# GpSimd makes the low halves of the activations in the second expert table's stage, VectorE only those of the weights

## The chip, the cores and the metric

The kernel runs on one core of a Trainium2 chip. The time is device microseconds of one launch of the whole program. Below, PE is TensorE, DVE is VectorE, ACT is ScalarE, POOL is GpSimd and SP is SyncE, whose queue issues most of the transfers.

## The reference

Two transformer blocks run on 256 tokens of width 1024, in 32-bit floating point. The first is an mLSTM mixer, an MLP and a gated per-layer embedding; the second is a forgetting attention beside an RWKV-7 time mix, then a layer of experts (PEER). The change is in the last part of that layer:

```
h = jax.nn.gelu(jnp.einsum('thkd,td->thk', u_table[idx], xb), approximate=False)
return jnp.einsum('thk,thkd->td', gate * h, v_table[idx])
x = _layer_norm(DN_ALPHA * x + _peer(x, ...), ln2_g[l], ln2_b[l])
```

There are 128 x 128 = 16384 experts, each with a row of `u_table` and a row of `v_table`. Every token chooses 16 experts in each of 8 heads. The kernel does not gather the rows. It computes the product of every expert with every token, multiplies it by a gate that is zero for the experts that were not chosen, and multiplies the result with the whole `v_table`.

## The kernel before

Every weight matrix is cut into items of 128 x 1024 numbers, 512 KB each, 442 in all. An item lands in one of four slots of the ring `RAW` (issued on SP's queue). Each fp32 product is made out of three faster matmuls: a number is split into a high half (rounded to the format fp32r) and a low half (the number less its high half), and high x high, low x high and high x low are summed in PSUM. So an item needs two more tiles of its own slot: `WH`, a cast on ACT, and `WL`, the subtraction `RAW - WH`. The semaphore `w_hi` counts the casts, `w_lo` the subtractions, and `w_used` the items that PE has finished. SP loads item n when item n-4 has been subtracted; ACT casts it when it has landed and PE has finished item n-4.

Up to the end of the first expert table (`u`, 128 items) POOL makes every `WL` (`split_low`, L335 to L340). After its last one POOL has no more work.

The stage of the second expert table (`v_table`, the last 128 items, here called 0 to 127) works otherwise. The left operand is the gated activation `HS[:, j, :]`, 128 experts x 256 tokens, and it has to be split too, into `CH` (a cast on ACT, `c_high`, L719 to L723) and `CL = HS - CH` (`c_low`, L785 to L789), each with four slots. For an item j, ACT makes `WH` and then `CH`; DVE makes `WL` (`v_low`, L1807 to L1811) and then `CL`; PE (`v_item`, L1191) waits for `w_lo` and for `cl_ready` and then runs 12 matmuls of 512 columns into four PSUM banks that gather the sum over all 128 items. The queues are in program order on each engine, and the loops are written out by hand:

- Entry. DVE's last gating work of the table before ends, then it runs `v_low(0)`, `c_low(0)`, `v_low(1)`, `c_low(1)` and so on to 3. `WH` of items 0 to 3 was already cast while DVE was still gating. ACT casts `CH` 0 to 3 only after the last gating, as `HS` is not final before it.
- First half, items 0 to 63. Only half of `HS` was gated in the table before. The gates of the other half (j from 64) come back from DRAM in 32 blocks into `stage`, fetched on ACT's queue, and DVE multiplies them in (`gate_rest`, L1779 to L1783), two blocks for every four items, ahead of the four `v_low` and `c_low` of the round.
- Middle, item 64. ACT casts `WH` of items 64 to 67, each of which waits for PE to finish the item four before it, then waits for the last `gate_rest`, issues the load of the saved residual, and only then casts `CH` of items 64 to 67 in a row.
- Second half, items 68 to 127. `WH`, `CH`, `WL`, `CL` for each item, nothing else.

At the end DVE and ACT do the last layer norm.

Of the kernel before, what the change touches and what calls it, by code (L numbers as in the profile page):

```python
# [19 lines left out]
ALU = mybir.AluOpType  # L20
# [30 lines left out]
PH, NK, TOPK = 8, 128, 16  # L51
# [16 lines left out]
RING = 4  # L68
# [35 lines left out]
def bass_blocks(nc, weights, x_in, p_in, vec_in, rows_in, gate_w_in, lora_in, mb_in, fb_in, out, rest_dram, x2_dram):  # L104
    with ExitStack() as ctx:
# [3 lines left out]
        def at(name, shape, dt, offset):  # L109
            return nc.alloc_sbuf_tensor_at(name, shape, dt, offset=base + offset)  # L110
# [100 lines left out]
        HS = at("HS", [P, NK, S], F32, A0)  # L211
# [22 lines left out]
        CH = at("CH", [P, RING, S], F32R, 8192)  # L234
        CL = at("CL", [P, RING, S], F32R, 12288)
# [9 lines left out]
        def sem(name):  # L245
            if name not in sems:
                sems[name] = ctx.enter_context(nc.semaphore(name))
            return sems[name]
# [8 lines left out]
        def plain(ap):  # L257
            return ap.bitcast(F32)
# [4 lines left out]
        @block.sync  # L263
        def _(sp):
            sp.dma_start(H[:, :, :], x_in.rearrange("(t p) d -> p t d", p=P)).then_inc(sem("x_landed"), 16)
            for n in range(RING):
                sp.dma_start(RAW[:, n, :], weights[n]).then_inc(w_landed[n], 16)
            full = (N_ITEMS // RING) * RING
            with sp.Fori(1, N_ITEMS // RING) as i:
                for slot in range(RING):  # L270
                    n = i * RING

                    sp.wait_ge(w_lo, n + (slot + 1 - RING))
                    sp.dma_start(RAW[:, slot, :], weights[bass.ds(n + slot, 1)].rearrange("a p d -> p (a d)")).then_inc(w_landed[slot], 16)
            for n in range(full, N_ITEMS):
                sp.wait_ge(w_lo, n + 1 - RING)
                sp.dma_start(RAW[:, n % RING, :], weights[n]).then_inc(w_landed[n % RING], 16)
            for t in range(NT):
                sp.wait_ge(sem("y_ready"), t + 1)
                sp.dma_start(out[t * P:(t + 1) * P, :], H[:, t, :]).then_inc(sem("y_stored"), 16)  # L280
            sp.wait_ge(sem("y_stored"), 16 * NT)


        @block.gpsimd
        def _(pool):
            made = sem("pool_made")
            count = [0]

            def link(ins):

                count[0] += 1
                ins.then_inc(made, 1)
                pool.wait_ge(made, count[0])

            def keep(view, pattern, base, cm, op, fill=0.0):
                link(nc.gpsimd.affine_select(out=view, in_=view, compare_op=op, fill=fill, base=base,  # L296
                                             pattern=pattern, channel_multiplier=cm))

            link(nc.gpsimd.memset(ident[:, :], 1.0))
            keep(ident[:, :], [[-1, P]], 0, 1, ALU.is_equal)  # L300
            nc.gpsimd.memset(ones_row[:, :], 1.0).then_inc(sem("ident_ready"), 1)
            link(nc.gpsimd.memset(sel4[:, :, :], 1.0))
            keep(sel4[:, :, :], [[-1, MH], [0, P]], 0, 1, ALU.is_equal)
            link(nc.gpsimd.memset(sel8[:, :, :], 1.0))
            keep(sel8[:, :, :], [[-1, FH], [0, P]], 0, 1, ALU.is_equal)

            link(nc.gpsimd.memset(mask_m[:, :, :, :], 1.0))
            for sb in range(NT):
                keep(mask_m[:, 0, sb, :], [[1, S]], -sb * P, -1, ALU.is_ge)
                keep(mask_m[:, 1, sb, :], [[-1, S]], sb * P, 1, ALU.is_ge)  # L310

            link(nc.gpsimd.memset(mask_f[:, :], 0.0))
            keep(mask_f[:, :], [[-1, S]], P, 1, ALU.is_ge, NEG)

            link(nc.gpsimd.memset(mask_r[:, :], 1.0))
            for half in range(2):
                v = mask_r[64 * half:64 * half + 64, :]
                keep(v[:, 0:64], [[1, 64]], -1, -1, ALU.is_ge)
                keep(v[:, 64:128], [[1, 64]], 0, -1, ALU.is_ge)
            link(nc.gpsimd.memset(blk_ones[:, :], 0.0))  # L320
            link(nc.gpsimd.memset(blk_ones[0:64, 0:64], 1.0))
            link(nc.gpsimd.memset(blk_ones[64:128, 64:128], 1.0))
            link(nc.gpsimd.memset(blk16[:, :], 1.0))
            for half in range(2):
                v = blk16[64 * half:64 * half + 64, :]
                keep(v, [[-BLK, 64 // BLK], [0, BLK]], 0, 1, ALU.is_ge)
                keep(v, [[BLK, 64 // BLK], [0, BLK]], BLK - 1, -1, ALU.is_ge)
            link(nc.gpsimd.memset(resets[:, :], 1.0))
            link(nc.gpsimd.memset(resets[:, :].rearrange("p (c t) -> p c t", t=CH_T)[:, :, 0:1], 0.0))
            link(nc.gpsimd.iota(iota_f[:, :], [[1, P]], base=0, channel_multiplier=0,  # L330
                                allow_small_or_imprecise_dtypes=True))
            link(nc.gpsimd.memset(eps_c[:, 1:2], GN_EPS))
            nc.gpsimd.memset(eps_c[:, 0:1], 1.0).then_inc(sem("consts_ready"), 1)

            def split_low(n, slot):  # L335


                pool.wait_ge(w_hi, n + 1)  # L338
                nc.gpsimd.tensor_tensor(WL[:, slot, :], RAW[:, slot, :], plain(WH[:, slot, :]),  # L339
                                        ALU.subtract).then_inc(w_lo, 1)  # L340

            full = FIRST["v_table"] // RING
            with pool.Fori(0, full) as i:  # L343
                for slot in range(RING):
                    split_low(i * RING + slot, slot)
            for n in range(full * RING, FIRST["v_table"]):
                split_low(n, n % RING)


        @block.scalar  # L350
        def _(act):
# [237 lines left out]
            for k, (_, _, dst, adds, _) in enumerate(INVERSE):  # L589
                if adds:  # L590
                    continue
                for half in range(2):
                    act.wait_ge(sem(f"inv_mm{half}"), k + 1)
                    b = 4 * (1 - half) + 2 * (k % 2)
                    nc.scalar.copy(inv[half][dst][:, :, :].rearrange("p u n -> p (u n)"),
                                   PS[:, b:b + 2, :].rearrange("p b n -> p (b n)")).then_inc(
                                       sem(f"inv_copied{half}"), 1)
# [615 lines left out]
        def _(dve):  # L1213
            V = nc.vector
# [564 lines left out]
            def gate_rest(i, b):  # L1779

                dve.wait_ge(sem(f"fetched{b}"), 16 * i + 16)
                hs = HS[:, NK // 2:NK, tokens(16 * i + 8 * b, 8)]
                V.tensor_tensor(hs, hs, stage[:, b, :, :], ALU.mult).then_inc(sem("rest_gated"), 1)  # L1783

            def c_low(j, c):

                dve.wait_ge(sem("ch_ready"), j + 1)
                hs = HS[:, j, :] if isinstance(j, int) else HS[:, bass.ds(j, 1), :].rearrange("p a s -> p (a s)")
                V.tensor_tensor(CL[:, c, :], hs, plain(CH[:, c, :]), ALU.subtract).then_inc(sem("cl_ready"), 1)  # L1789


            wait("u_bank_free", NT + NK // 4)
            wait("x2_stored", 16)
# [13 lines left out]
            def v_low(j, c):  # L1807

                slot = (FIRST["v_table"] + c) % RING
                dve.wait_ge(w_hi, j + (FIRST["v_table"] + 1))  # L1810
                V.tensor_tensor(WL[:, slot, :], RAW[:, slot, :], plain(WH[:, slot, :]), ALU.subtract).then_inc(w_lo, 1)  # L1811
# [2 lines left out]
            dve.wait_ge(w_lo, FIRST["v_table"])  # L1814
            for c in range(4):
                v_low(c, c)
                c_low(c, c)
            with dve.Fori(0, S // 16) as i:
                for b in range(2):
                    gate_rest(i, b)  # L1820
                for c in range(4):
                    v_low(4 * i + RING + c, c)
                    c_low(4 * i + RING + c, c)
            with dve.Fori(S // 16 + 1, NK // 4) as i:
                for c in range(4):
                    v_low(4 * i + c, c)
                    c_low(4 * i + c, c)

            used(N_ITEMS - 1)
            wait("x2_back", 16)  # L1830
# [76 lines left out]
```

## Time and profile before

| | |
|---|---|
| median of 3 runs | 1645.95 us (1644.81 to 1646.76) |
| the profiled execution, its own time | 1643.69 us |
| its span, from the first to the last instruction | 1641.6 us |
| outside the span | 2.09 us |
| PE, DVE, ACT and POOL busy | 1519.2, 869.9, 750.6 and 777.8 us |
| the stage of the second expert table, first to last matmul | 1276.54 to 1628.9 us |

The span is longer than any engine's busy time, so an engine's own total does not tell what sets the end. Busy PE is not PE at its peak, as matmuls are pipelined; where they follow each other without a gap, PE is what the rest waits for. The page gives POOL no busy time in the last quarter of the span.

### The profile page before, as it was taken

The numbers are of one execution on the slowest core, as the hardware profiler recorded it, in microseconds if no ns is written. First come the engines' busy times: TensorE is split into PE (matmuls) and PEld (weight loads), VectorE is DVE, ScalarE is ACT, GpSimd is POOL, SyncE is SP. The second block draws the span as 40 slices with busy tenths as digits, with TensorE's granted clock in tenths as the row PEclk, the third lists the DMA queues.
The fourth block names the chain that finished last, engine by engine and source line by source line (L and its number), as shares of the span: only waits on it lengthen the run. The fifth ranks groups of instructions, "written<-read, shape, count | busy, mean of one in ns | idle before, by whom it ended". The sixth has DMA issues, their size and how long they took to land.

```text
span 1641.6 us, 28210 instructions
## 1 busy us (share of the span) xinstructions
PE 1519.2 (93%) x9610; PEld 1360.0 (83%) x9610; DVE 869.9 (53%) x1889; ACT 750.6 (46%) x1064; POOL 777.8 (47%) x346
## 2 busy tenths in 40 slices
PE   6987999987999798977999999999999999999996
PEld 5766999865997568855999999999999788878885
DVE  3234442012927643234249980688888666665554
ACT  5354555344448223233456666333333444545543
POOL 6834688865776300125769998666664000000000
PEclk9998999998999668988999999999999999999998
DMA  4532455544454200015445556555554777766562
GB/s 165 181 101 81 138 181 192 192 142 140 153 169 134 83 1 1 27 40 166 167 149 171 185 167 197 167 169 177 172 179 147 262 243 242 248 219 193 191 195 85
DMA packets 74644, 254.99 MB, mean 155 GB/s; under 512 B 8409, under 2 KB 8793, under 8 KB 74330
## 3 DMA queue, kind: packets, MB, share of 16 engines
q1 hardware_dynamic: 63632, 231.76, 43.7%
q10 hardware_dynamic: 10954, 22.43, 4.0%
q8 instruction: 40, 0.66, 0.2%
q14 instruction: 18, 0.15, 0.0%
HBM read 243.67 MB, written 10.49 MB: 155 GB/s over the span
## 4 chain that ended last, share of the span: by engine, by line
PE 37%; issue 35%; POOL 26%; DVE 1%; DMA 1%; POOLq 1%; ACT 0%; ACTq 0%; DVEq 0%; SPq 0%
PE PS L787 34%; POOL WL L339 25%; PE PS L1154 3%; DMA stage<-gates_rest 0%; POOLq L343 0%; POOLq L338 0%; DMA RAW<-weights 0%; DVE H L1834 0%; ACT LNS L634 0%; POOL sel L296 0%; POOL mask_m L296 0%; DVE hot_j L1761 0%; DVE H L1683 0%; ACT L389 0%; POOL blk L296 0%
## 5 line engine op out<-in xcount | busy, mean ns | idle before, releaser
L339 POOL TENSOR_TENSOR WL<-RAW,WH 128x1024 fp32r<-128x1024 f32 x310 | 766.0, 2480 | 480.5 <-ACT WH L359 384.7
L787 PE MATMUL PS<-XH,WH 128*128 128x256 f32 x1648 | 472.5, 287 | 4.3 <-POOL WL L339 2.2
L787 PE MATMUL PS<-XH,WL 128*128 128x256 f32 x1648 | 466.4, 283 | 0.0
L787 PE MATMUL PS<-XL,WH 128*128 128x256 f32 x1648 | 466.4, 283 | 0.0
L688 ACT CAST WH<-RAW 128x1024 fp32r<-128x1024 f32 x252 | 265.0, 1051 | 393.5 <-PE PS L787 381.1
L787 PEld LDWEIGHTS PS<-XH,WH 128*128 128x128 f32 x1648 | 316.3, 192 | 5.5 <-issue 2.6
L787 PEld LDWEIGHTS PS<-XL,WH 128*128 128x128 f32 x1648 | 316.4, 192 | 0.0
L787 PEld LDWEIGHTS PS<-XH,WL 128*128 128x128 f32 x1648 | 316.1, 192 | 0.0
L359 ACT CAST WH<-RAW 128x1024 fp32r<-128x1024 f32 x186 | 194.2, 1050 | 155.4 <-PE PS L787 150.8
L787 PE MATMUL PS<-WH,CH 128*128 128x512 f32 x512 | 200.1, 391 | 5.3 <-DVE CL L1789 5.3
L787 PE MATMUL PS<-WL,CH 128*128 128x512 f32 x512 | 199.7, 390 | 0.0
L787 PE MATMUL PS<-WH,CL 128*128 128x512 f32 x512 | 199.7, 390 | 0.0
L1811 DVE TENSOR_TENSOR WL<-RAW,WH 128x1024 fp32r<-128x1024 f32 x128 | 156.4, 1222 | 80.2 <-ACT WH L688 80.2
L1760 DVE TENSOR_SCALAR hot_i<-PS,IT 128x128 f32<-128x128 f32 x256 | 88.0, 344 | 87.0 <-PE PS L1154 44.2
L787 PEld LDWEIGHTS PS<-WH,CH 128*128 128x128 f32 x512 | 96.5, 188 | 26.0 <-issue 3.4
L787 PEld LDWEIGHTS PS<-WL,CH 128*128 128x128 f32 x512 | 96.6, 189 | 20.0
L787 PEld LDWEIGHTS PS<-WH,CL 128*128 128x128 f32 x512 | 96.5, 188 | 19.9
L1761 DVE TENSOR_SCALAR hot_j<-PS,JT,GT 128x128 f32<-128x128 f32 x256 | 102.8, 401 | 0.0
L787 PE MATMUL PS<-WH,XH 128*128 128x512 f32 x240 | 97.6, 407 | 5.6 <-POOL WL L339 5.6
L787 PE MATMUL PS<-WL,XH 128*128 128x512 f32 x240 | 95.8, 399 | 0.0
L787 PE MATMUL PS<-WH,XL 128*128 128x512 f32 x240 | 95.3, 397 | 0.0
L1154 PE MATMUL PS<-hot_j,hot_i 128*128 128x128 f32 x512 | 67.9, 275 | 0.5 <-DVE hot_j L1761 0.4
(368 smaller groups left out, 1913.9 us busy)
## 6 DMA issues: line engine op xcount, KB each, us to landing
RAW<-weights SPq DMA_DIRECT2D x438, 512.0 KB, 3.5
gates_rest<-stage ACTq DMA_DIRECT2D x32, 256.0 KB, 4.2
stage<-gates_rest ACTq DMA_DIRECT2D x32, 256.0 KB, 4.7
H<-x SPq DMA_DIRECT2D x1, 1024.0 KB, 5.5
LG<-rows ACTq DMA_DIRECT2D x2, 512.0 KB, 4.7
LB<-rows ACTq DMA_DIRECT2D x2, 512.0 KB, 6.2
x<-H ACTq DMA_DIRECT2D x1, 1024.0 KB, 3.9
H<-x ACTq DMA_DIRECT2D x1, 1024.0 KB, 4.9
```

Of the source, the lines that this page charges most:

```text
L339: nc.gpsimd.tensor_tensor(WL[:, slot, :], RAW[:, slot, :], plain(WH[:, slot, :]), ALU.subtract).then_inc(w_lo, 1)
L359: nc.scalar.copy(WH[:, slot, :], RAW[:, slot, :]).then_inc(w_hi, 1)
L688: nc.scalar.copy(WH[:, slot, :], RAW[:, slot, :]).then_inc(w_hi, 1)
L787: last = mm(dst, a, b, start=start and k == 0, stop=stop and k == len(pairs) - 1)
L1154: last = mm(PS[:, 4 + c, k * NK:(k + 1) * NK], hot_i[:, g, a, :], hot_j[:, g, a, :], start=True, stop=True)
L1760: V.tensor_scalar(hot_i[:, g, a, :], iota_ps, at_token(IT, t), None, ALU.is_equal)
L1761: last = V.tensor_scalar(hot_j[:, g, a, :], iota_ps, at_token(JT, t), at_token(GT, t), ALU.is_equal, ALU.mult)
L1811: V.tensor_tensor(WL[:, slot, :], RAW[:, slot, :], plain(WH[:, slot, :]), ALU.subtract).then_inc(w_lo, 1)
```

## The change

`c_low` moves from the block of DVE to the end of the block of POOL, as a loop over all 128 items. It waits for the same semaphore, computes the same subtraction and signals the same semaphore as before. DVE keeps `gate_rest` and `v_low`. Nothing on ACT, PE or SP is changed.

```
@@ gpsimd, behind the last split_low
+            def c_low(j, c):
+                pool.wait_ge(sem("ch_ready"), j + 1)
+                hs = HS[:, bass.ds(j, 1), :].rearrange("p a s -> p (a s)")
+                nc.gpsimd.tensor_tensor(CL[:, c, :], hs, plain(CH[:, c, :]), ALU.subtract).then_inc(sem("cl_ready"), 1)
+
+            with pool.Fori(0, NK // 4) as i:
+                for c in range(4):
+                    c_low(4 * i + c, c)
@@ vector
-            def c_low(j, c):
-                dve.wait_ge(sem("ch_ready"), j + 1)
-                hs = HS[:, j, :] if isinstance(j, int) else HS[:, bass.ds(j, 1), :].rearrange("p a s -> p (a s)")
-                V.tensor_tensor(CL[:, c, :], hs, plain(CH[:, c, :]), ALU.subtract).then_inc(sem("cl_ready"), 1)
...
             for c in range(4):
                 v_low(c, c)
-                c_low(c, c)
             with dve.Fori(0, S // 16) as i:
                 for b in range(2):
                     gate_rest(i, b)
                 for c in range(4):
                     v_low(4 * i + RING + c, c)
-                    c_low(4 * i + RING + c, c)
             with dve.Fori(S // 16 + 1, NK // 4) as i:
                 for c in range(4):
                     v_low(4 * i + c, c)
-                    c_low(4 * i + c, c)
```

## Rows read from the trace of the kernel before

**Rows 1.** The page, its first line.

```profile
span 1641.6 us, 28210 instructions
```

**Rows 2.** Windows: both halves of the stage; busy us (count) of each engine, PEclk, DMA share.

```profile
1276.50:1452.40 175.90, 175.86 (x768) 145.24 (x768) 115.97 (x159) 84.99 (x125) 0.00 (x0) 0.99 0.75 246
1454.50:1628.90 174.40, 174.35 (x768) 144.09 (x768) 97.86 (x127) 81.72 (x121) 0.00 (x0) 1.00 0.57 183
```

**Rows 3.** Timeline of PE, three starts after an idle time: start, us, idle, releaser.

```profile
52.57 0.77 PE L787 MATMUL PS<-WH,XH 128*128 128x512 f32 x1 [3.67 <-POOL WL L339]
...
1276.54 0.77 PE L787 MATMUL PS<-WH,CH 128*128 128x512 f32 x1 [3.21 <-DVE CL L1789]
...
1454.48 0.50 PE L787 MATMUL PS<-WH,CH 128*128 128x512 f32 x1 [2.08 <-DVE CL L1789]
```

**Rows 4.** Timeline of DVE at the entry: items 0, 0, 1, and 4.

```profile
1274.04 1.23 DVE L1811 TENSOR_TENSOR WL<-RAW,WH 128x1024 fp32r<-128x1024 f32 x1
1275.96 0.42 DVE L1789 TENSOR_TENSOR CL<-HS,CH 128x256 fp32r<-128x256 f32 x1 [0.70 <-ACT CH L722]
1276.31 1.22 DVE L1811 TENSOR_TENSOR WL<-RAW,WH 128x1024 fp32r<-128x1024 f32 x1
...
1287.36 0.42 DVE L1789 TENSOR_TENSOR CL<-HS,CH 128x256 fp32r<-128x256 f32 x1
```

**Rows 5.** Timeline of ACT at the entry, then in the middle (items 67 and 64 to 67).

```profile
1275.53 1.02 ACT L722 CAST CH<-HS 128x256 fp32r<-128x256 f32 x3 [1.52 <-issue]
...
1452.49 1.04 ACT L688 CAST WH<-RAW 128x1024 fp32r<-128x1024 f32 x1 [1.67 <-PE PS L787]
...
1453.44 1.32 ACT L722 CAST CH<-HS 128x256 fp32r<-128x256 f32 x4
```

**Rows 6.** Timeline of DVE in the middle, item 64.

```profile
1448.32 1.22 DVE L1811 TENSOR_TENSOR WL<-RAW,WH 128x1024 fp32r<-128x1024 f32 x1
1454.00 0.42 DVE L1789 TENSOR_TENSOR CL<-HS,CH 128x256 fp32r<-128x256 f32 x1 [4.46 <-ACT CH L722]
```

**Rows 7.** Timeline of ACT and of DVE in the second half, one item.

```profile
1591.76 0.40 ACT L722 CAST CH<-HS 128x256 fp32r x1
...
1591.89 1.22 DVE L1811 TENSOR_TENSOR WL<-RAW,WH 128x1024 fp32r<-128x1024 f32 x1 [1.16 <-ACT WH L688]
1593.04 0.42 DVE L1789 TENSOR_TENSOR CL<-HS,CH 128x256 fp32r<-128x256 f32 x1
```

**Rows 8.** Groups of POOL's instructions by shape: count, busy us, mean ns.

```profile
L339 POOL TENSOR_TENSOR WL<-RAW,WH 128x1024 fp32r<-128x1024 f32 x310 | 766.0, 2480 | 480.5 <-ACT WH L359 384.7 <-ACT WH L688 95.5
...
L307 POOL MEMSET mask_m<- 128x1024 f32 x1 | 1.0, 956 | 0.1
...
L312 POOL MEMSET mask_f<- 128x256 f32 x1 | 0.3, 316 | 0.1
```

**Rows 9.** Single lines (ns min/median/max, first and last start) and DVE's timeline beside POOL.

```profile
L339 POOL TENSOR_TENSOR WL<-RAW,WH x59: 2396/2402/2410, 1040.1 to 1258.5; 128x1024 fp32r<-128x1024 f32 x59
...
865.54 2.28 DVE L1716 TENSOR_TENSOR cand<-tv 128x2048 f32<-128x2048 f32 x1
L339 POOL TENSOR_TENSOR WL<-RAW,WH x2: 2409/3326/4244, 863.0 to 865.8; 128x1024 fp32r<-128x1024 f32 x2
...
897.34 4.42 DVE L1728 TENSOR_TENSOR tmp<-iota_f,bbf 128x2048 f32<-128x2048 f32 x1
L339 POOL TENSOR_TENSOR WL<-RAW,WH x2: 4437/4440/4443, 899.6 to 904.0; 128x1024 fp32r<-128x1024 f32 x2
...
L1489 DVE TENSOR_SCALAR T<-T,vec x4: 341/2372/2424, 532.2 to 539.2; 128x256 f32<-128x256 f32 x4
```

**Rows 10.** Windows: PE after the three idle times of rows 3, columns as in rows 2.

```profile
52.50:57.60 5.10, 5.03 (x12) 4.00 (x13) 0.00 (x0) 0.34 (x1) 5.10 (x3) 0.50 0.60 204
...
1276.50:1279.60 3.10, 3.06 (x7) 2.48 (x8) 3.10 (x5) 0.35 (x2) 0.00 (x0) 0.50 0.88 192
...
1454.40:1457.50 3.10, 3.02 (x13) 2.53 (x14) 3.10 (x6) 0.36 (x2) 0.00 (x0) 1.00 0.93 366
```

## The prediction, made before the changed kernel ran

> **What bounds the kernel now.** I read the span first [rows 1]: 1641.6 us, of which only the stage of the second expert table, from 1276.54 on, is touched. Then the windows of its two halves [rows 2]: PE is busy for 175.86 of 175.90 us and for 174.35 of 174.40 us, 768 matmuls in each, while DVE has 116 and 98 us of work, ACT 85 and 82, POOL none. So inside the halves no operand is ever late. Without a gap a matmul takes 174.35 / 768 = 0.227 us and an item of 12 takes 2.72 us. Then the timeline of PE for what is left [rows 3]: two idle times, 3.21 us at the entry and 2.08 us in the middle, both ended by `CL` on DVE. A third loss hides behind the first: the 7 matmuls after it run at half the granted clock (0.50, 1.2 GHz) for 3.1 us [rows 10], and come 0.43 us apart. After the 2.08 us idle time the clock is whole (1.00). Half of 3.1 us is lost, 1.55 us. So all that this stage could give back is 3.21 + 2.08 + 1.55 = 6.8 us; DVE's load is not part of it.
>
> Both idle times end in the same way: ACT casts the first `CH` late, DVE subtracts for `CL`, PE starts. This is the instruction that moves. In the entry `CH(0)` is cast from 1275.53 (three casts in 1.02 us, the first done at about 1275.93) [rows 5], DVE makes `CL(0)` from 1275.96 to 1276.38 [rows 4], PE starts at 1276.54. In the middle `CH(64)` is cast from 1453.44 to about 1453.84 [rows 5], `CL(64)` runs from 1454.00 to 1454.42 [rows 6], PE starts at 1454.48.
>
> **What is removed.** DVE loses 128 subtractions of 0.42 us, 54 us of work. They lie beside a PE that never waits for DVE within the halves [rows 2], so this is worth 0. Item 4 shows the tightest cover: PE reaches it after 7 slow matmuls and 41 of 0.227 us, at 1279.6 + 9.3 = 1288.9, and its `CL` ended at 1287.78 [rows 4], 1.1 us earlier. `gate_rest` waits for its transfer, not for DVE, and comes no later than before. `v_low(1)` to `v_low(3)` finish up to 1 us earlier, so SP issues the loads of items 5 to 7 that much earlier. These queue on SP behind the load of item 4, which is issued after `v_low(0)` as before; I take 0 for it, and the 1.1 us cover a delay of the blocks fetched on ACT's queue. PE, ACT and SP issue the same instructions and transfers as before.
>
> **What is added.** POOL gets 128 subtractions of 128x256, a shape that the trace doesn't have on POOL. Call its time X. The same operation on 128x1024 takes 2.40 us [rows 9], its memsets 0.956 us for 1024 and 0.316 us for 256 columns [rows 8], which is 0.10 us fixed and the rest in proportion. With 0.1 to 0.2 us fixed, X is 0.68 to 0.75; I take 0.70. The lower bound is the memset of this width, 0.32; the upper is the whole 2.40, if nothing shrank with the width. The memset pair speaks against that end, as it shrank to a third. PE starts 0.1 us behind POOL's end as behind DVE's, so this changes nothing.
>
> **What the two engines do to each other.** Beside DVE's work of the first expert table, which reads PSUM, POOL's subtraction keeps its 2.402 us (59 of them, 2396 to 2410 ns) [rows 9]. But `v_low` reads two SBUF tiles, and rows with that show another picture. At 865.54 DVE starts an addition of two SBUF inputs that lasts 2.28 us, to 867.82; POOL's subtraction starts at 865.85 and takes 4.24 us, to 870.09. This is DVE's end plus 2.27 us: POOL stood still until DVE was done, and only 0.13 us of its 2.40 passed meanwhile. At 897.34 it is DVE that starts behind POOL, and an operation of the same size takes 4.42 us instead of 2.28; POOL's next ones take 4.44 each. So one waits for the whole of the other's instruction, and they take turns. DVE's four unlinked scalar operations at 532.2, with a median of 2.37 us and a minimum of 0.34, show that POOL also gets its turn between DVE instructions that follow in a row.
>
> The entry by this: `v_low(0)` starts at 1274.04, and the next instruction of DVE's comes 1.15 us behind a `v_low`'s start (1591.89 and 1593.04 [rows 7]). So with `c_low(0)` gone `v_low(1)` runs from 1275.19 to 1276.41, where before it started at 1276.31. `CL(0)` is ready to go at 1275.97 and stands until 1276.41, then needs X - 0.13. It ends at 1276.98 instead of 1276.38: X - 0.10 = **0.60 us** later.
>
> The middle: `WH(67)` is cast from 1452.49 to 1453.53, after PE's last matmul of item 63 [rows 5]. `WH` of 65 and 66 were ready earlier, and DVE, which stood before `c_low(64)` for 4.46 us [rows 6], now works them off while it would have waited. So at 1453.57 it is free for `v_low(67)` and holds until 1454.79. `CL(64)` could go at 1453.88, 0.3 us too late, and ends at 1454.79 + X - 0.13 = 1455.36 instead of 1454.42: X + 0.24 = **0.94 us** later. PE's idle time becomes 2.08 + 0.94 = 3.02 us. The next items follow with room: `CL(65)` about 0.6 us behind, where PE takes 2.72 us for item 64.
>
> Then the clock. An idle time of 2.08 us left it whole; 3.21 us and 3.67 us were followed by 3.1 and 5.1 us at 1.2 GHz [rows 3, 10]. 3.02 us lies much nearer to those, so I take a slow stretch of 3.1 us in the middle too: **1.55 us** more. Its bounds are 0 and half of 5.1, 2.55 us. The entry's idle time grows from 3.21 to 3.81 us; its slow stretch may grow to 5.1 us, at most 1.0 us; I take 0.
>
> Everywhere else the collision is hidden. In the second half `CH` ends at 1592.16, `v_low` of 1591.89 holds until 1593.11, and `CL` ends near 1593.68 instead of 1593.46 [rows 7]; PE uses an item three items (8 us) after its `WH` could be cast. Per item the two need 1.22 + 0.57 of 2.72 us.
>
> Sum: 0.60 + 0.94 + 1.55 = 3.1 us. The profiled execution would go from 1643.69 (span 1641.6 and 2.09 outside it) to 1646.8, and the median of the runs, 2.26 us above it, from 1645.95 to **1649.0 us**.
>
> The Trainium skill says the same of the port as a rule: on its page "SBUF — State Buffer", section "SBUF: two separate sides", VectorE and GpSimd share one pair of ports, and a VectorE instruction with two SBUF inputs and a GpSimd instruction that reads SBUF exclude each other for a whole instruction. It speaks against this change, and it is what the rows from 865 on show; by the 59 undisturbed subtractions alone, which it explains as reads of PSUM on VectorE's side, the sum would be the 0.5 us of the second rival.
>
> **Rivals.**
> - The second slow stretch doesn't come: 3.02 us is still under the 3.21 that had one. Then 0.60 + 0.94 = 1.5 us, 1647.5.
> - No collision: the engines run beside each other. `CL(0)` ends at 1275.97 + 0.70, 0.29 later, `CL(64)` at about 1454.6, 0.2 later: 0.5 us, 1646.4. The 59 subtractions speak for it, the 4.24 and 4.44 us against it.
> - On the other side, clearly slower: POOL is not let in between `v_low(1)`, `(2)` and `(3)`. They overlap by 0.07 us, where DVE's two-input operations near 900 wait for one another. Then `CL(0)` starts when `v_low(3)` ends, 1274.04 + 3 x 1.15 + 1.22 = 1278.71, and ends at 1279.28, 2.9 us later than before, 2.3 more than in the sum; with the longer slow stretch (1.0) the sum is 6.4 us, 1652.3. It passes 0.2% as soon as `CL(0)` ends after 1277.2. The scalar operations at 532.2 speak against it.
> - The port becomes the bound. That needs 1.22 + X above 2.72, so X above 1.5; at 2.40 it would cost 0.9 x 128 = 115 us. Only the memsets speak against it, but clearly.
> - Faster: `CL` would have to come earlier, and it hangs on `CH` from ACT, which isn't moved. Earlier loads would have to shorten a wait of PE's, and none of its two is for a load. Even half of the 6.8 us is out of sight.
>
> **How the numbers follow.** 0.2% is 3.3 us, about what a measurement of this kernel can tell from no change; the three runs lie 1.95 us apart. The forecast (both stalls longer, second slow stretch) gets 0.45; without the slow stretch 0.22; no collision 0.10; POOL not let in, or the slow stretches at their upper bounds (3.1 + 1.0 + 1.0 = 5.1 us), 0.15; the port as bound 0.02; faster by any way 0.03; other slower ways 0.03. The range goes from below the case without collision, less half a microsecond and more of spread, 1645.5, to just past the third rival, 1652.5. The forecast's own 3.1 us lies at the edge of 0.2%, so its 0.45 falls in two: 0.25 within, 0.20 beyond. Within 0.2%: 0.25 + 0.21 + 0.10 = 0.56. Slower: 0.20 + 0.01 + 0.15 + 0.02 + 0.03 = 0.41. Faster: 0.03.
>
> **What would show it.** POOL's `CL` group: 128 instructions, near 1.4 us each in the second half (0.95 of it standing), though 0.70 where DVE is idle; `v_low` still 1.22 us there. PE's idle times 3.8 and 3.0 us, both ended by `CL` on POOL, and the granted clock 0.50 behind both. `v_low(67)` ends just before `CL(64)` gets going. Both halves still 2.72 us for each item. I am wrong if `CL` takes 0.70 us everywhere, if `CL(0)` ends behind `v_low(3)`, or if PE waits anywhere inside a half.

## The result and the profile after

The changed kernel takes 1649.53 us (median of 17 runs, 1646.72 to 1650.49), the kernel before 1645.78 us in runs beside them (17, 1641.92 to 1648.68). The ratio is 1.0022, with a 95% interval from 1.0014 to 1.0029: 2.3 to 4.8 us slower. The forecast was 3.1 us slower, 1649.0 us, with a range from 1645.5 to 1652.5. Of the experiments below, one run of e4 (6340 us) and one of e7 (5597 us) are far off all others and not in the ratios.

The page of the changed kernel, its first line and the two groups of the stage's subtractions:

```profile
span 1647.9 us, 28283 instructions
...
L353 POOL TENSOR_TENSOR CL<-HS,CH 128x256 fp32r<-128x256 f32 x128 | 164.0, 1283 | 200.4 <-ACT CH L732 200.4
...
L1815 DVE TENSOR_TENSOR WL<-RAW,WH 128x1024 fp32r<-128x1024 f32 x128 | 163.5, 1294 | 117.8 <-ACT WH L698 117.3
```

`CL` takes 1.28 us on average on GpSimd, against 0.42 on VectorE; `WL` has gone from 1222 to 1294 ns, as at the entry and in the first half some of them now stand behind a `CL` (the 60 from 1464.9 on take 1224 to 1226 ns). In the answers for the tile `CL` and for `WL`'s line (ns min/median/max) one sees how much of this is waiting:

```profile
L353 POOL TENSOR_TENSOR CL<-HS,CH x128: 722/1380/1827, 1278.0 to 1625.9; 128x256 fp32r<-128x256 f32 x128
```

```profile
L1815 DVE TENSOR_TENSOR WL<-RAW,WH x128: 1210/1224/1766, 1276.0 to 1625.4; 128x1024 fp32r<-128x1024 f32 x128
```

The shortest `CL`, 0.722 us, is the subtraction alone. The median of 1.380 is one that stands for 0.66 us. The timeline of one item in the second half (ScalarE, VectorE, GpSimd), to be held against [rows 7]:

```profile
1595.39 0.40 ACT L732 CAST CH<-HS 128x256 fp32r x1
...
1595.52 1.23 DVE L1815 TENSOR_TENSOR WL<-RAW,WH 128x1024 fp32r<-128x1024 f32 x1 [1.49 <-ACT WH L698]
...
1595.96 1.38 POOL L353 TENSOR_TENSOR CL<-HS,CH 128x256 fp32r<-128x256 f32 x1 [1.34 <-ACT CH L732]
```

`WL` holds until 1596.75, `CL` ends at 1597.34: 0.59 us behind it. That is the 0.72 us less 0.13, the same arithmetic as for the long subtraction at 865 [rows 9].

Now the two places where PE waits, on PE's timeline, against [rows 3]:

```profile
1279.06 0.77 PE L797 MATMUL PS<-WH,CH 128*128 128x512 f32 x1 [3.81 <-POOL CL L353]
...
1459.27 0.80 PE L797 MATMUL PS<-WH,CH 128*128 128x512 f32 x1 [3.03 <-POOL CL L353]
```

3.81 us at the entry and 3.03 us in the middle; the forecast had 3.81 and 3.02. The two engines there, first VectorE's and GpSimd's row of the entry (four items merged in each), then the middle:

```profile
1275.97 5.70 DVE L1815 TENSOR_TENSOR WL<-RAW,WH 128x1024 fp32r<-128x1024 f32 x4
...
1278.04 4.91 POOL L353 TENSOR_TENSOR CL<-HS,CH 128x256 fp32r<-128x256 f32 x4 [15.19 <-ACT CH L732]
...
1457.40 1.23 DVE L1815 TENSOR_TENSOR WL<-RAW,WH 128x1024 fp32r<-128x1024 f32 x1 [1.49 <-ACT WH L698]
...
1457.85 3.42 POOL L353 TENSOR_TENSOR CL<-HS,CH 128x256 fp32r<-128x256 f32 x4 [9.55 <-ACT CH L732]
```

At the entry `WL(1)` ends at about 1278.34, and `CL(0)`, which lasts 0.87 us from 1278.04, ends at 1278.91, 0.57 us behind it. In the middle `WL(67)` got in at 1457.40 and holds until 1458.63. `CL(64)`, with its start at 1457.85, ends at 1459.21, again 0.58 us behind it. Four `WL` in a row at the entry take 5.70 us instead of 3 x 1.15 + 1.22 = 4.7, so there VectorE stands behind GpSimd in its turn. Last, windows for the clock behind the two idle times, and for the rest of both halves, columns as in [rows 10]:

```profile
1279.00:1285.10 6.10, 6.04 (x14) 4.79 (x15) 2.67 (x2) 0.29 (x1) 3.95 (x3) 0.50 0.99 340
1459.20:1462.70 3.50, 3.44 (x8) 2.77 (x9) 0.00 (x0) 0.00 (x0) 2.08 (x4) 0.51 0.99 366
...
1285.10:1455.90 170.80, 170.80 (x755) 141.39 (x753) 111.21 (x95) 84.35 (x123) 72.94 (x60) 1.00 0.72 242
1462.70:1634.90 172.20, 172.20 (x761) 142.52 (x760) 73.48 (x60) 81.42 (x120) 82.77 (x60) 1.00 0.52 173
```

PE runs at 1.2 GHz (0.50) for 14 matmuls, 6.1 us, at the entry, twice as long as before, and for 8 matmuls in the middle, where it didn't before. In the rest it doesn't wait once: the collisions of the other items cost nothing.

The sum for the two profiled executions: 0.60 + 0.95 us of longer idle time; the 14 slow matmuls lose 2.9 us where 7 lost 1.5, 1.4 more; the 8 in the middle lose 1.6. That is 4.5 us in the stage. One term is missing from it: outside the span the changed kernel has 1.75 us on average of its 17 runs, where before had 2.09. All kernels below with the loop on GpSimd have 1.7, all others 2.1, so about 0.35 us come back there; the traces don't show why. The spans differ by 6.3; another 1.9 us lie ahead of it (PE stops for the entry at 1275.25 instead of 1273.33), in code that the change doesn't touch, so one pair of executions is no measure of a few microseconds. The medians are, within their intervals.

### The profile page after: what moved, and what is told of

It is laid out like the page before. It is cut to its first block, busy times and chain, and to the rows that moved or that the text cites. A ratio compares the mean times of both kernels' runs of the same rounds, so it can differ in the third digit from the quotient of the medians.

```text
span 1647.9 us, 28283 instructions
## 1 busy us (share of the span) xinstructions
PE 1523.7 (92%) x9610; PEld 1363.3 (83%) x9610; DVE 845.3 (51%) x1761; ACT 750.5 (46%) x1064; POOL 941.8 (57%) x474
## 4 chain that ended last, share of the span: by engine, by line
PE 38%; issue 35%; POOL 26%; POOLq 1%; DVE 0%; ACT 0%; ACTq 0%; DVEq 0%
PE PS L797 34%; POOL WL L339 25%; PE PS L1164 3%; POOLq L343 0%; POOLq L338 0%; DVE H L1835 0%; ACT LNS L644 0%; POOL CL L353 0%; POOL sel L296 0%; POOL mask_m L296 0%; DVE H L1693 0%; ACT L399 0%; DVE hot_j L1771 0%; DVEq L105 0%; DVE hot_i L1770 0%
## 5 line engine op out<-in xcount | busy, mean ns | idle before, releaser
L353 POOL TENSOR_TENSOR CL<-HS,CH 128x256 fp32r<-128x256 f32 x128 | 164.0, 1283 | 200.4 <-ACT CH L732 200.4
L1815 DVE TENSOR_TENSOR WL<-RAW,WH 128x1024 fp32r<-128x1024 f32 x128 | 163.5, 1294 | 117.8 <-ACT WH L698 117.3
```

What stands on the lines that cost most here:

```text
L353: nc.gpsimd.tensor_tensor(CL[:, c, :], hs, plain(CH[:, c, :]), ALU.subtract).then_inc(sem("cl_ready"), 1)
```

## The experiments

Each kernel ran 11 or 12 times beside 15 to 35 runs of the kernel before. Ratios are against those, with 95% intervals; 0.001 is 1.6 us. "Slow matmuls" are those that come 0.43 us apart, at 1.2 GHz; one of them loses 0.2 us. The counts take in matmuls at the ends of a stretch that are only partly slow, so 7 to 10 of them stand for one and the same length, some 3 us.

The runs of this section also have their mean granted clock on record, and the spread of the run times goes with it. Of the 112 runs of the kernel before, the 27 with 0.950 took 1647.0 us on average and the 27 with 0.953 took 1643.9: about 1 us for each 0.001. So executions of one kernel differ in how long PE runs at 1.2 GHz, in this stage or elsewhere. The profile of each kernel is a single execution. That of e2 (1652.9 us) is the longest of its twelve, and those of e1 (1649.1), e5 (1644.0), e6 (1646.8), e7 (1646.6) and e12 (1647.1) lie 2.2 to 3.7 us above the medians of their kernels; their waits can be relied on, their slow stretches less.

**e1: GpSimd goes first where it matters.** On the changed kernel, in VectorE's block (for the second place the last round of the loop is written out):

```
             for c in range(4):
+                if c == 1:
+                    wait("cl_ready", 1)
                 v_low(c, c)
...
+            for c in range(4):
+                if c == 3:
+                    wait("cl_ready", NK // 2 + 1)
+                v_low(NK // 2 + c, c)
```

> The changed kernel, in which VectorE holds back two of its subtractions: WL(1) until CL(0) is done, and WL(67) until CL(64) is done. Theory (one waits for the whole of the other's instruction): both subtractions on GpSimd now take 0.72 us, PE's idle times shrink from 3.81 and 3.03 to 3.5 and 2.3 us, and the slow stretch after the middle one goes away (0.8 + 0.7 + 1.55 in all), so the time is 0.5 to 1.5 us above the kernel before, about 1646.8. Rival (GpSimd is merely slow to start or to signal, whatever VectorE does): both idle times stay at 3.8 and 3.0, and the time 3.7 us above before.

Ratio 1.0004 (0.9992 to 1.0015). PE's timeline of this kernel, then the line of `CL` between 1278.0 and 1278.8 (two instructions):

```profile
1278.96 0.77 PE L797 MATMUL PS<-WH,CH 128*128 128x512 f32 x1 [3.66 <-POOL CL L353]
...
1458.59 0.50 PE L797 MATMUL PS<-WH,CH 128*128 128x512 f32 x1 [2.39 <-POOL CL L353]
```

```profile
L353 POOL TENSOR_TENSOR CL<-HS,CH x2: 726/728/729, 1278.1 to 1278.8; 128x256 fp32r<-128x256 f32 x2
```

With VectorE held back `CL(0)` takes 0.73 us instead of 0.87, and the wait in the middle shrinks from 3.03 to 2.39 us, nearly all of the 0.7 expected. So the instruction on the other engine is what `CL` stood behind. At the entry only 0.15 of the 0.3 us expected come back: `CL(0)` starts 0.59 us after the first cast (1277.50 to 1278.09), in the changed kernel too (1277.45 to 1278.04), where VectorE's started after 0.43 us (1275.53 to 1275.96). So of the 0.60 us of longer idle time there the collision is 0.15; 0.30 is the slower subtraction and 0.15 the later start, which the wait for `WL(1)` hides in the changed kernel. The slow matmuls did not go as expected: 14 at the entry and 9 in the middle, those after only 2.39 us of idle time. The run medians favour the theory; the profile does not, and it is of an execution 3.7 us above the median. By the ratios e1 is 3 us faster than the changed kernel, with an interval of about 2 us to either side, and its idle times are 0.8 us shorter.

**e2 and e3: one half each.** On GpSimd only items 64 to 127 (e2), or only 0 to 63 (e3), the rest on VectorE. Only the loop on GpSimd is shown, against that of the changed kernel; VectorE's loops are divided to match:

```
e2, gpsimd
+            pool.wait_ge(sem("cl_ready"), NK // 2)
-            with pool.Fori(0, NK // 4) as i:
+            with pool.Fori(NK // 8, NK // 4) as i:
e3, gpsimd
-            with pool.Fori(0, NK // 4) as i:
+            with pool.Fori(0, NK // 8) as i:
```

> CL on GpSimd for items 64 to 127 only, on VectorE before. Theory: the entry is as before (PE idle 3.2 us), the middle as after the change (3.0 us, then 3.1 us at 1.2 GHz): 0.95 + 1.55 = 2.5 us above before, 1648.3. Rival (the middle costs only its longer wait and the rest is in the entry): 0.95 above.

> CL on GpSimd for items 0 to 63 only, on VectorE from 64. Theory: the entry is as after the change (PE idle 3.8 us, the slow stretch up to 5.5 us long), the middle as before (2.1 us, clock whole): 0.6 us and up to 1.2 us from the longer slow stretch, 0.6 to 1.8 above before, about 1647.0. Rival (the first half costs time elsewhere, as gate_rest and WL now wait for GpSimd): PE waits inside the first half, or more than 2 us above.

e2: ratio 1.0003 (0.9993 to 1.0012), less than the 2.5 us expected. e3: 1.0023 (1.0014 to 1.0032), 3.8 us, more than the 0.6 to 1.8 expected, and as much as the whole change. PE waits at no other place in its stage, so the rival of e3 that the first half costs by waits is out; its other form, more than 2 us above before, came true. PE's timelines, the entry and the middle of e2, then of e3:

```profile
1282.13 0.47 PE L798 MATMUL PS<-WH,CH 128*128 128x512 f32 x1 [3.21 <-DVE CL L1800]
1461.14 0.80 PE L798 MATMUL PS<-WH,CH 128*128 128x512 f32 x1 [3.03 <-POOL CL L353]
```

```profile
1277.99 0.76 PE L797 MATMUL PS<-WH,CH 128*128 128x512 f32 x1 [3.81 <-POOL CL L353]
1457.22 0.50 PE L797 MATMUL PS<-WH,CH 128*128 128x512 f32 x1 [2.02 <-DVE CL L1799]
```

The idle times are those of the kernel whose code stands at that place (2.02 against 2.08 us in the middle of e3, the others to the hundredth). What differs is the clock: in e3 14 slow matmuls at the entry, and 9 in the middle after 2.02 us, where the profile of before had none after 2.08; in e2 9 at the entry and 14 in the middle. The runs say the same: the granted clock is 0.9494 on average over the runs of e3, 0.9518 over those of before beside them and 0.9525 over e2's. At 1 us for each 0.001, an estimate from the 112 runs above, some 2.5 us of e3's cost are clock, while e2 had slightly less of it than before.

**e4: the kernel before with a late `CL(64)`.**

```
                 v_low(NK // 2 + c, c)
+                if c == 0:
+                    wait("ch_ready", NK // 2 + 1)
+                    V.memset(late[:, :], 0.0)
                 c_low(NK // 2 + c, c)
```

> The kernel before with nothing on GpSimd; VectorE clears a dead tile of 128x768 between CH(64) and CL(64), which makes CL(64) some 0.8 us later. Theory (a longer idle time alone brings the slow stretch): PE's idle time in the middle is 2.9 us, then 3.1 us at 1.2 GHz, 2.3 us above before in all, 1648.1. Rival (the slow stretch has to do with GpSimd, or 2.9 us are too short for it): 0.8 us above before and a whole clock.

Ratio 1.0004 (0.9995 to 1.0013). PE waited 2.70 us in the middle, and the clock stayed whole. The rival holds for this profile: 2.70 us alone don't bring a slow stretch with certainty. The ratio fits it too: 0.7 us above before.

**e5: the middle reordered, on the kernel before.** ScalarE no longer casts four `WH`, of which each waits for PE, ahead of `CH(64)`:

```
             for c in range(4):
                 split_high_dyn(V0, NK // 2 + c, c)
-            act.wait_ge(sem("rest_gated"), S // 8)
-            act.dma_start(H[:, :, :].rearrange("p t d -> p (t d)"), x2_dram).then_inc(sem("x2_back"), 16)
-            for c in range(4):
-                c_high(NK // 2 + c, c)
+                if c == 1:
+                    act.wait_ge(sem("rest_gated"), S // 8)
+                if c:
+                    c_high(NK // 2 + c - 1, c - 1)
+            c_high(NK // 2 + 3, 3)
+            act.dma_start(H[:, :, :].rearrange("p t d -> p (t d)"), x2_dram).then_inc(sem("x2_back"), 16)
```

> The kernel before, in which ScalarE casts CH(64) as soon as WH(65) is cast and the last gates are in, and CH(65) to CH(67) each one place behind, so that CH(64) no longer waits for PE to finish item 63. Theory: PE's idle time of 2.08 us in the middle is gone and with it any slow stretch after it: 2.1 us below before if before seldom has one there, up to 3.7 us if often. Rival (something else, the last gates or a load, is due next): a wait of PE's stays in the middle, by another releaser.

Ratio 0.9980 (0.9969 to 0.9991), 3.3 us faster than before. PE's only wait in the stage is the 3.21 us of the entry, with 8 slow matmuls. 2.1 us is the idle time, which lies within the interval (1.5 to 5.1 us). The other 1.2 would fit a kernel before that often has a slow stretch in the middle. The mean clock of the runs points that way (0.9532 in e5, 0.9518 in before beside it), and of three profiles with this wait (before, e6, e3) one has it, e3's. How often is not shown.

**e9: the same edit on the changed kernel.**

> The changed kernel with the middle reordered as in e5. Theory (the move costs where PE waits for a CL, and only there): PE doesn't wait in the middle; what is left over e5 is the entry, 0.6 us of longer idle time and about one more slow unit of 1.5 us: 2.1 us above e5, about 1644.5, 0.7 below before. Rival (the halves themselves are slower with GpSimd in the stage): 3.5 us or more above e5.

Ratio 0.9992 (0.9983 to 1.0001): 2.0 us above e5 (0.9992 less 0.9980), as expected, though the two intervals together leave it anywhere from nothing to 4 us. The two profiles are the cleanest pair here, as PE stops for the entry at the same time in both (1276.04 and 1276.00). Their spans are 1643.9 and 1641.9 us, 2.0 apart, and the whole difference lies at the entry:

```profile
1279.85 0.77 PE L799 MATMUL PS<-WH,CH 128*128 128x512 f32 x1 [3.81 <-POOL CL L353]
```

3.81 us and 14 slow matmuls, against 3.21 us and 8 in e5, then not one wait to the end of the stage: 0.60 + 1.4 = 2.0 us.

**e6, e7, e8: the entry reordered,** on the kernel before (e6), with the middle too (e7), and both on the changed kernel (e8). Only the moved lines are shown, at their new places:

```
scalar
+            act.wait_ge(w_used, FIRST["v_table"])
+            act.wait_ge(sem("gated"), S // 4)
+            nc.scalar.copy(CH[:, 0, :], HS[:, 0, :]).then_inc(sem("ch_ready"), 1)
             park(S // 16 - 1, 1)
vector
+            dve.wait_ge(w_lo, FIRST["v_table"])
+            v_low(0, 0)
             gate(S // 16 - 1, 3)
```

> The kernel before, in which VectorE makes WL(0) ahead of its last gating, and ScalarE casts CH(0) ahead of three transfers that it issues. Theory: PE starts the stage 1.3 us earlier (idle 3.2 to 1.9), and the slow stretch after the idle time, 1.5 to 2.9 us of loss in the profiles so far, is shorter or gone: 1.3 to 4.2 us below before. Rival (the slow stretch comes after any idle time near 2 us as well): 1.3 us below.

> Both reorderings on the kernel before. Theory: the sum of the two, 3.4 to 7 us below before, near 1640.5. Rival: less than 2 us below, if the stalls' time comes back later.

> Both reorderings on the changed kernel. Theory (the move costs time only where PE stands waiting for a CL): in the middle nothing is left of its cost; in the entry CL(0) on GpSimd still stands until WL(1) is through, about 0.9 us, so it is 0.9 us above the same reordering of the kernel before, and at least 2 us below before. Rival (the move costs time within the halves too): 3 us or more above the reordered kernel before.

e6: 0.9997 (0.9988 to 1.0006), 0.5 us below before where 1.3 or more was expected. e7 and e8: 0.9986 (0.9977 to 0.9995) each, 2.3 us below, where the theory for e7 had 3.4 to 7 and the rival under 2. PE's timeline of e7:

```profile
1294.16 0.50 PE L790 MATMUL PS<-WH,CH 128*128 128x512 f32 x1 [2.59 <-DVE CL L1792]
```

The entry's wait shrank from 3.21 to 1.96 us as planned, and not one slow matmul followed it in this profile. But item 4 was now due before it was ready, and PE waited 2.59 us there (1.06 in e6, where a slow stretch had held it up). `CL(4)` stands on VectorE behind two `gate_rest` that wait for their transfers, VectorE's timeline of e7:

```profile
1290.36 0.69 DVE L1786 TENSOR_TENSOR HS<-HS,stage 128x512 f32 x1 [5.68 <-DMA stage<-gates_rest]
1291.94 0.69 DVE L1786 TENSOR_TENSOR HS<-HS,stage 128x512 f32 x1 [0.89 <-DMA stage<-gates_rest]
1292.55 1.22 DVE L1813 TENSOR_TENSOR WL<-RAW,WH 128x1024 fp32r<-128x1024 f32 x1
1293.69 0.42 DVE L1792 TENSOR_TENSOR CL<-HS,CH 128x256 fp32r<-128x256 f32 x1
```

In e8 `CL(4)` is on GpSimd and behind nothing, yet `WL(4)` still waits for the gates; its profile has two matmuls at that place that are late, by 0.35 us together. There the moved `CL` loses 0.7 us at the entry (2.67 against 1.96 us of idle time) and does not have the wait at item 4. Against each other e7 and e8 are level; the 0.9 us between them that was expected is not seen.

**e10 and e11: also the layer norm's rows loaded later,** on e8 (with the held-back `WL(1)` of e1) and on e7:

```
-            act.dma_start(LG2[:, :], rows_in[4:5, :].broadcast_to([P, D])).then_inc(sem("ln2_landed"), 16)
-            act.dma_start(LB2[:, :], rows_in[5:6, :].broadcast_to([P, D])).then_inc(sem("ln2_landed"), 16)
...
             act.dma_start(H[:, :, :].rearrange("p t d -> p (t d)"), x2_dram).then_inc(sem("x2_back"), 16)
+            act.dma_start(LG2[:, :], rows_in[4:5, :].broadcast_to([P, D])).then_inc(sem("ln2_landed"), 16)
+            act.dma_start(LB2[:, :], rows_in[5:6, :].broadcast_to([P, D])).then_inc(sem("ln2_landed"), 16)
```

> e8 (the changed kernel, entry and middle reordered) in which also WL(1) is held back until CL(0) is done, and the two rows of the last layer norm, 1 MB, are loaded in the middle instead of at the entry. Theory: PE's idle time at the entry 2.2 us (CL(0) no longer stands), and the fetched gates and the load of item 4 land sooner, so nothing waits at item 4: 1 to 3 us below e8, 1640 to 1641.5. Rival (the MB is in nobody's way): as e8, 1642.5.

> e7 (the kernel before, entry and middle reordered) with the two rows of the last layer norm loaded in the middle. Theory: the wait of 2.6 us at item 4, where CL(4) on VectorE stands behind two gate_rest that wait for their transfers, is gone or under 0.5 us: 2 to 3 us below e7, about 1640.5, and level with e10, since then neither engine's CL is behind anything. Rival: the wait at item 4 stays and e10 is the faster by it.

e10: 0.9980 (0.9971 to 0.9989). e11: 0.9982 (0.9973 to 0.9991). The wait at item 4 is gone in e10 and down to two late matmuls (0.6 us) in e11, and the two are level as expected. But neither is 2 us below its parent; within the intervals e5, e7, e8, e10 and e11 are one time, 2.3 to 3.3 us below before.

**e12: e5 with the entry's idle time filled.**

```
+            pe.wait_ge(w_hi, V0 + 1)
+            for k in range(11):
+                mm(PS[:, 2, :], WH[:, V0 % RING, 0:P], WH[:, V0 % RING, 0:512], start=True, stop=True)
             for c in range(4):
                 v_item(c, c, start=(c == 0))
```

> e5 (the kernel before with the middle reordered) in which PE runs 11 matmuls with no use, into a free PSUM bank, while it would stand at the entry. Theory (the slow stretch follows from PE's idle time): the idle time shrinks from 3.2 to 0.7 us, PE's first item runs at 2.4 GHz, 1.5 us below e5, about 1640.5. Rival (the slow stretch there has another cause, as the kind of work or the start of the stage): 1.5 us are lost as before, 1642.

Ratio 0.9998 (0.9989 to 1.0008): 3.0 us slower than e5, where 1.5 us faster was expected. PE's timeline, and windows behind both starts:

```profile
1280.07 0.47 PE L789 MATMUL PS<-WH,CH 128*128 128x512 f32 x1 [0.68 <-DVE CL L1794]
...
1293.11 0.50 PE L789 MATMUL PS<-WH,CH 128*128 128x512 f32 x1 [1.88 <-DVE CL L1794]
```

```profile
1280.00:1283.10 3.10, 3.03 (x13) 2.55 (x14) 3.10 (x5) 0.39 (x2) 0.00 (x0) 1.00 0.96 186
1293.30:1297.00 3.70, 3.70 (x10) 2.88 (x10) 3.70 (x5) 0.65 (x2) 0.00 (x0) 0.54 0.77 245
```

The mechanism was right: with 0.68 us of idle time the clock stays at 2.4 GHz behind the entry. The price was not. PE reached item 4 some 1.5 us earlier, waited there for 1.88 us, and had its slow stretch after that. The earlier arrival is not all of it. VectorE's second `gate_rest`, ahead of `WL(4)`, waited for its transfer, in e12 and in e5:

```profile
1290.89 0.69 DVE L1788 TENSOR_TENSOR HS<-HS,stage 128x512 f32 x1 [2.80 <-DMA stage<-gates_rest]
```

```profile
1288.25 0.69 DVE L1785 TENSOR_TENSOR HS<-HS,stage 128x512 f32 x1 [1.29 <-DMA stage<-gates_rest]
```

That is 14.0 us after PE had stopped at the entry in e12 (at 1276.86, the filling matmuls left out) and 12.25 us in e5 (at 1276.00). Whether the filling or chance made the transfer 1.8 us later, no run tells.

## Why the prediction was right

**Where it costs.** Both places, and only these: PE waits at the entry and in the middle for `CL` on GpSimd, and nowhere else. e5 and e9 divide the cost: the middle is worth 0.0030 in the changed kernel (1.0022 less 0.9992), 4.9 us, and 0.0020, 3.3 us, in the one before; so the move costs 1.6 us there, and 2.0 us at the entry (e9 less e5). Each is a difference of ratios and uncertain by 2 to 3 us, and the two add up to the whole (0.0022) by construction. e2 and e3 divide it otherwise, 0.5 us (-1.2 to 2.0) and 3.8 us (2.3 to 5.3). These are measured apart, and their sum of 4.3 us agrees with the measured 3.75 (each with 1.5 us to either side), so there is no sign of a third place. How it divides is not settled. Idle time and clock ran apart there: by the profiles the two places have 0.60 and 0.95 us more of idle time, and the rest is slow matmuls, of which by the mean clocks e3's runs had more than before and e2's no more.

**The size of the added subtraction.** 0.70 us was taken, 0.72 measured. With 2.40 us for 1024 columns that is a fixed part of 0.16 us, within the 0.1 to 0.2 that was allowed; the pair of memsets alone had 0.10.

**The collision.** The step "one waits for the whole of the other's instruction" gave 0.60 and 0.94 us; measured 0.60 and 0.95. e1 shows it from the other side: the same subtraction takes 0.73 us when VectorE is held back. The 0.60 us of the entry holds as a sum; the standing is only 0.15 us of it, where the prediction had 0.31 (0.60 less the 0.29 of its rival without a collision). In the middle it is 0.64 (3.03 less e1's 2.39), as forecast. That they take turns was also right. The rival in which GpSimd is not let in between three `WL` would have had `CL(0)` end 2.9 us later; it ended 0.6 us later. The rival without a collision falls with the median `CL` of 1.38 us.

**The clock: right in kind, mis-sized in one term.** For the entry the prediction said of the slow stretch that it "may grow to 5.1 us, at most 1.0 us; I take 0". It grew to 6.1 us in each of the three profiles with 3.81 us of idle time (the changed kernel, e3, e9), 14 matmuls against 7 or 8, and lost 1.4 us more. The forecast's 1.55 us for the middle is 1.6 us in the profiled execution. But it was the difference to a kernel before that was believed to have no slow stretch there. If e5's extra 1.2 us are such stretches, it often has one, and the change adds less than the whole: of the 1.6 us for the middle, 0.95 is idle time and 0.65 is left for the clock, 0.9 less than was taken. The 0.35 us less outside the span was not in the sum either. These errors have opposite signs, 1.4 us too little and some 1.3 too much, so that 3.1 us came so near to 3.75 is in part luck; the idle times are not. The larger chance, 0.56, was for a change within 0.2%. The measured 0.22% (0.14 to 0.29) lies on that line.

**The 6.8 us that the stage could give back** were not to be had. e7 and e12 show that part of the slow stretch and of the idle time at the entry covers a wait for item 4, which is due next (in e12 with a later transfer beside it). What these runs gained is no more than the middle alone gave.

## What to carry to other kernels

A 0.42 us instruction on an engine that is at most 66% busy cost nothing here as long as its consumer never waited for it. What counts in moving it is the few places where the consumer does wait, and there a slower engine loses. Before moving work to GpSimd, look at what VectorE runs at that moment: with two SBUF inputs on both sides the later one stood for the rest of the earlier (the 0.72 us subtraction ended 0.57 to 0.59 us behind a `WL`, the 2.40 us one 2.27 us behind an addition), so price it as that instruction's remainder plus its own time less 0.13 us. And for a stall, look at the order on the engine in front of it: e5, which only casts `CH(64)` ahead of two casts that wait for PE, gave 3.3 us, about what the move lost.

## What the runs showed of the hardware

A slow stretch at 1.2 GHz came in two sizes here: some 3 us, 7 to 10 matmuls, or some 6 us, 14 or 15. By the idle time of PE ahead of it, each number one place in one profile:

| idle time, us | no slow matmul | 7 to 10 | 14 or 15 |
|---|---|---|---|
| 0.35 to 1.06 | 0.35 (e11), 0.68 (e12), 1.06 (e6) | | |
| 1.88 to 2.08 | 1.96 (e7), 2.08 (before, e6) | 1.88 (e12), 1.96 (e6), 1.97 (e11), 2.02 (e3) | |
| 2.35 to 2.70 | 2.59 (e7), 2.70 (e4) | 2.35 (e10), 2.39 (e1), 2.67 (e8) | |
| 3.03 | | the changed kernel | e2 |
| 3.21 | | before, e4, e5, e2 | |
| 3.66 and 3.81 | | | e1, the changed kernel, e3, e9 |

In the seven cases below 3 us, and in e2's of 3.21 us, the stretch began only 0.3 to 1.3 us after PE had started again. So for idle times of 2 to 3 us one profile can't tell whether a kernel pays for the clock. Only many runs can, and a prediction should carry both outcomes.
